# Four blocks of a depthwise convolution on 128x32 stationary tiles with time-shifted copies

## The reference, cut to what matters

```python
def causal_dwconv(x, w, b):
    width, ch = w.shape
    y = lax.conv_general_dilated(
        x, w[:, None, :].astype(x.dtype), window_strides=(1,),
        padding=((width - 1, 0),), dimension_numbers=("NWC", "WIO", "NWC"),
        feature_group_count=ch)
    return y + b

def conformer_conv(u, b_glu, w_dw, b_dw, ln_g, ln_b):
    u = u + b_glu
    a, gate = jnp.split(u, 2, axis=-1)
    v = a * jax.nn.sigmoid(gate)
    v = causal_dwconv(v, w_dw, b_dw)
    v = layernorm(v, ln_g, ln_b)
    return jax.nn.silu(v)
```

## Time and profile before

| | before |
|---|---|
| time, median of 3 runs | 1257.6 us (1256.13 to 1257.68) |
| span of the profiled execution | 1251.5 us, 19242 instructions |
| PE busy | 1209.8 us, 97% |
| DVE busy | 894.0 us, 71% |
| ACT busy | 639.7 us, 51% |
| POOL busy | 14.0 us, 1% |
| granted TensorE clock, mean | 0.995 |

### The profile page before, as it was taken

One profiled execution on the slowest core, in us unless ns is written; L12 is line 12 of the kernel. 1 busy time (PEld: TensorE's weight loads), 2 busy tenths in 40 slices (PEclk: granted clock), 3 DMA queues, 4 the chain that ended last, 5 costly groups with the idle time before them and its releaser, 6 DMA issues.

```text
span 1251.5 us, 19242 instructions
## 1 busy us (share of the span) xinstructions
PE 1209.8 (97%) x7928; PEld 1092.5 (87%) x7928; DVE 894.0 (71%) x1369; ACT 639.7 (51%) x1017; POOL 14.0 (1%) x32
## 2 busy tenths in 40 slices
PE   6999899999999999999999999999999999999997
PEld 6988798999989869899998978878798989999885
DVE  5996678877776666788778856665576647677664
ACT  6564555555464435555555334435444555555553
POOL 0000000000000000000000000000000000000000
PEclk9999999999999999999999999999999999999999
DMA  9520435555443323465454544544454732223341
GB/s 387 220 101 1 168 135 174 213 186 187 183 169 123 105 86 126 157 214 198 174 201 137 205 164 157 205 168 146 173 186 174 259 147 102 102 102 102 135 178 58
DMA packets 28710, 200.52 MB, mean 160 GB/s; under 512 B 3408, under 2 KB 3536, under 8 KB 5072
## 3 DMA queue, kind: packets, MB, share of 16 engines
q1 hardware_dynamic: 28624, 199.30, 43.8%
HBM read 198.24 MB, written 1.05 MB: 159 GB/s over the span
## 4 chain that ended last, share of the span: by engine, by line
PE 80%; DVE 11%; ACT 5%; issue 3%; DMA 1%; DVEq 0%; POOLq 0%; ACTq 0%; POOL 0%; SPq 0%
PE bank L726 22%; PE bank L727 22%; PE bank L728 22%; DVE WL L1616 4%; ACT WH L1236 3%; PE bank L874 2%; DVE work L1808 2%; PE bank L1210 1%; PE bank L1193 1%; PE bank L1107 1%; PE bank L860 1%; DVE work L1761 1%; DVE work L1757 1%; PE bank L937 1%; PE bank L1184 1%
## 5 line engine op out<-in xcount | busy, mean ns | idle before, releaser
L1616 DVE TENSOR_TENSOR WL<-RAW,WH 128x2048 fp32r<-128x2048 f32 x180 | 411.5, 2289 | 151.2 <-ACT WH L1236 150.1
L1236 ACT ACTIVATE WH<-RAW 128x2048 fp32r<-128x2048 f32 x180 | 343.2, 1910 | 208.5 <-PE bank L728 202.8
L726 PE MATMUL bank<-XH,WH 128*128 128x256 f32 x1264 | 361.9, 286 | 18.1 <-DVE WL L1828 12.0
L727 PE MATMUL bank<-XL,WH 128*128 128x256 f32 x1264 | 358.6, 284 | 0.0
L728 PE MATMUL bank<-XH,WL 128*128 128x256 f32 x1264 | 358.5, 284 | 0.0
L726 PEld LDWEIGHTS bank<-XH,WH 128*128 128x128 f32 x1264 | 243.4, 193 | 22.5 <-DVE XL L1821 11.9
L727 PEld LDWEIGHTS bank<-XL,WH 128*128 128x128 f32 x1264 | 243.4, 193 | 0.5
L728 PEld LDWEIGHTS bank<-XH,WL 128*128 128x128 f32 x1264 | 243.4, 193 | 0.0
L726 PE MATMUL bank<-WH,MH 128*128 128x512 f32 (+1 forms) x544 | 199.7, 367 | 5.7 <-DVE WL L1616 3.8
L727 PE MATMUL bank<-WL,MH 128*128 128x512 f32 (+1 forms) x544 | 196.7, 362 | 0.0
L728 PE MATMUL bank<-WH,ML 128*128 128x512 f32 (+1 forms) x544 | 196.6, 361 | 0.0
(11 more groups left out here) (275 smaller groups left out, 1507.0 us busy)
## 6 DMA issues: line engine op xcount, KB each, us to landing
RAW<-wstream SPq DMA_DIRECT2D x181, 1024.0 KB, 4.8
con<-consts SPq DMA_DIRECT2D x1, 1681.0 KB, 13.2
work<-xT_in SPq DMA_DIRECT2D x1, 1024.0 KB, 4.9
x<-x_in SPq DMA_DIRECT2D x1, 1024.0 KB, 11.0
work<-mem_in SPq DMA_DIRECT2D x1, 1024.0 KB, 16.3
xn<-memT_in SPq DMA_DIRECT2D x1, 1024.0 KB, 11.9
par<-params SPq DMA_DIRECT2D x1, 858.0 KB, 14.2
gfree<-g_final SPq DMA_DIRECT2D x1, 512.0 KB, 17.0
```

Source lines behind the costliest of these rows:

```text
L726: mm(o, ah, bh, start=start, stop=False)
L727: mm(o, ah, bl, start=False, stop=False)
L1236: act_fn(WH[:, t % RING, :], RAW[:, t % RING, :], ACT.Copy).then_inc(w_rounded, 1)
L1616: tt(WL[:, t % RING, :], RAW[:, t % RING, :], WH[:, t % RING, :].bitcast(F32), ALU.subtract).then_inc(w_split, 1)
```

## The change

Blocks 2 to 5 now go to TensorE in full, blocks 0 and 1 stay on VectorE (62 taps). The stationary tile is 128x32: for a group of 32 channels its 128 rows are four copies of these channels, the copy n shifted by n tokens, and it holds the four taps 4m to 4m+3 as four stacked 32x32 diagonals. A block takes eight such steps (m = 0 to 7; the 32nd tap is zero) for each of its four groups, so 32 matmuls, and 128 in all. The four groups of a block write the four quarters of the partitions of one bank. Within a step the groups follow each other, then comes the next step. Slot 0 does the whole of block 2, the other six slots half a block each.

The shifted copies are made by DMA from `vpad` (`shift`), 16 DMAs of 32 partitions x 572 columns for each pair of blocks, one pair into MH, ML, the other into XH, XL. The SP queue issues them between the loads of weight tiles, behind waits on a new semaphore `glu_done`, the second pair also behind TensorE's use of XH in `qm`. The stationary tiles are made by GpSimd: four small additions form `pick`, and one `tensor_tensor` of 128x1024 for each block (`conv_weights`) multiplies it by the taps from the parameter array, whose part `w_rep` replaces four blocks of `w_dw_a`. They lie in the place of the diagonals, in `gfree` and in `xn`. The two `rms` of GpSimd now stand between them. ScalarE builds no diagonals, and takes the four convolution results out of PSUM with the bias (`conv_outs`). The mean takes the blocks in the order 2, 3, 4, 0, 1, 5. The load of `gfree` moves to the first tile of the second block.

```diff
-PE_CONV = {3: CONV // 2, 4: CONV, 5: CONV}
-PE_TAPS = [(b, k) for b, n in PE_CONV.items() for k in range(n)]
-TAPS_PER_SLOT = 11
+PE_BLOCKS = (2, 3, 4, 5)
+SHIFTS = 4
+GROUPS = 4
+STEPS = 8
+DIAG = P // SHIFTS
+VREP = 2 * (CONV - 1 + T)
+CONV_SLOTS = {0: [(2, 0), (2, 1)], 1: [(3, 0)], 2: [(3, 1)], 3: [(4, 0)], 4: [(4, 1)], 5: [(5, 0)], 6: [(5, 1)]}
...
+            def shift(j):
+
+                sp.wait_ge(glu_done, j)
+                for n in range(SHIFTS):
+                    for g in range(GROUPS):
+                        at = 2 * j * (CONV - 1 + T) + n
+                        sp.dma_start(shifted(j, g)[DIAG * n:DIAG * (n + 1), :], vflat[DIAG * g:DIAG * (g + 1), at:at + VREP])\
+                            .then_inc(shifts_loaded[j - 1], 16)
...
+                if TILES[t] == ("mk", 1):
+                    shift(1)
+                if TILES[t] == ("o0", O0_ORDER[0]):
+                    sp.wait_ge(w_used, TILE[("qm", 0)] + 1)
+                    shift(2)
+                if TILES[t] == FOX_FIRST[0]:
+
+                    sp.wait_ge(w_used, TILE[("o0", O0_ORDER[-1])] + 1)
                     sp.dma_start(gfree[:, :], g_final.partition_broadcast(P)).then_inc(gf_loaded, 16)
...
-            for n in (1, 0):
-                rms(n)
+            pool.wait_ge(ident_loaded, 16)
+            link(nc.gpsimd.tensor_tensor(pick[:, :], ident[:, 0:DIAG], ident[:, DIAG:2 * DIAG], ALU.add))
...
+            def conv_weights(b):
+
+                n = GROUPS * STEPS
+                taps = col("w_rep", PE_BLOCKS.index(b) * n, n)
+                nc.gpsimd.tensor_tensor(conv_w[b], pick[:, :].unsqueeze(1).to_broadcast([P, n, DIAG]),
+                                        taps.unsqueeze(2).to_broadcast([P, n, DIAG]), ALU.mult).then_inc(conv_w_built, 1)
+
+            rms(1)
+            pool.wait_ge(par_loaded, 16)
+            pool.wait_ge(front_lo, KD)
+            conv_weights(2)
+            rms(0)
+            conv_weights(3)
+            pool.wait_ge(front_lo, 2 * KD)
+            conv_weights(4)
+            conv_weights(5)
...
-                for n in range(slot * TAPS_PER_SLOT, (slot + 1) * TAPS_PER_SLOT):
-                    b, k = PE_TAPS[n]
-                    if k == 0:
+                for b, part in CONV_SLOTS[slot]:
+                    j = b // 2
+                    if part == 0:
                         conv_out[b] = take(("cv", b))
-                    last = k == PE_CONV[b] - 1
-                    pe.wait_ge(diag_built, n + 1)
-                    mm(conv_out[b][:, 0:T], diag[:, n % DIAGS, :], vpad[:, b, k:k + T], start=(k == 0), stop=last)\
-                        .then_inc(aux_done if last else diag_used, 1)
+                        pe.wait_ge(conv_w_built, PE_BLOCKS.index(b) + 1)
+                        if b % 2 == 0:
+                            pe.wait_ge(shifts_loaded[j - 1], 16 * SHIFTS * GROUPS)
+                    for m in range(STEPS // 2 * part, STEPS // 2 * (part + 1)):
+                        for g in range(GROUPS):
+                            at = (b % 2) * (CONV - 1 + T) + SHIFTS * m
+                            last = mm(conv_out[b][DIAG * g:DIAG * (g + 1), 0:T], conv_w[b][:, g * STEPS + m, :],
+                                      shifted(j, g)[:, at:at + T], start=(m == 0), stop=(m == STEPS - 1))
+                    if part == 1:
+                        last.then_inc(aux_done, 1)
...
-            for at, b in enumerate((0, 1, 4, 2, 3, 5)):
-                pe.wait_ge(*dve_a.next())
+            for at, b in enumerate((2, 3, 4, 0, 1, 5)):
+                if b in PE_BLOCKS:
+                    is_free(pe, ("cv", b))
+                else:
+                    pe.wait_ge(*dve_a.next())
...
+            def conv_outs(slot):
+
+                for b, part in CONV_SLOTS.get(slot, []):
+                    if part == 1:
+                        ready(act, ("cv", b))
+                        free(act_fn(conv[:, b, :], B(("cv", b))[:, 0:T], ACT.Identity, bias=col("b_dw_a", b)), ("cv", b), "act")
...
-            TAPS_IN_SLOT = 10
+            TAPS_IN_SLOT = 4
             dve_taps = [(b, i) for i in range(CONV) for b in (0, 1)]
-            dve_taps += [(b, i) for i in range(CONV) for b in (2, 3) if not 0 < i <= PE_CONV.get(b, 0)]
```

More of the change, by code:

```diff
@@ L384, in program @@
         hmask = sb("hmask", [P, 2])
+        pick = sb("pick", [P, DIAG])
         WORK = 10464
@@ L432, in program, with shifted @@
         z = wk(8448, NMB, T)
-        DIAGS = TAPS_PER_SLOT
-        diag = wk(8448, DIAGS, P)
+        xn_flat = xn[:, :, :].rearrange("p i d -> p (i d)")
+        conv_w = {b: v.rearrange("p (n c) -> p n c", c=DIAG)
+                  for b, v in zip(PE_BLOCKS, (wk(8448, 1024), gfree[:, :], xn_flat[:, 0:1024], xn_flat[:, 1024:2048]))}
+        def shifted(j, g):
+            part = (MH, ML)[g // 2][:, 0:6, :] if j == 1 else (XH, XL)[g // 2][:, :, :]
+            at = (g % 2) * VREP
+            return part.rearrange("p a t -> p (a t)").bitcast(F32)[:, at:at + VREP]
         fy = wk(0, 2, 4 * T)
@@ L508, in program @@
         ms_done = sem("ms_done")
-        diag_built = sem("diag_built")
-        diag_used = sem("diag_used")
+        glu_done = sem("glu_done")
+        shifts_loaded = [sem("shifts_loaded1"), sem("shifts_loaded2")]
+        conv_w_built = sem("conv_w_built")
         rstd_done = sem("rstd_done")
@@ L665, in halved @@
                 nc.gpsimd.tensor_tensor(rhalf[:, n, :], rstd[:, n, :], half[:, :], ALU.mult).then_inc(half_done, 1)
-            for n in (1, 0):
-                rms(n)
+            pool.wait_ge(ident_loaded, 16)
+            link(nc.gpsimd.tensor_tensor(pick[:, :], ident[:, 0:DIAG], ident[:, DIAG:2 * DIAG], ALU.add))
+            for n in (2, 3):
+                sync()
+                link(nc.gpsimd.tensor_tensor(pick[:, :], pick[:, :], ident[:, n * DIAG:(n + 1) * DIAG], ALU.add))
+            sync()
+            def conv_weights(b):
[12 more added lines that the diff above has]
+            conv_weights(5)
             pool.wait_ge(ln_var_done, 1)
@@ L1317, in attention @@
                             values(j)
-                    if base == 0 and s + 1 < n + 3:
-                        diags(s + 1)
+                    if base == 0:
+                        conv_outs(s - 1)
                     if s < n:
@@ L1848, in _ @@
                 else:
-                    ins.then_inc(dve_for_pe, 1)
+                    ins.then_inc(glu_done, 1)
+                    dve.wait_ge(glu_done, j)
                 if j == 0:
@@ L1874, in _ @@
                 dve.drain().then_inc(dve_for_pe, 1)
-            ready(dve, ("cv", 3))
-            dve.wait_ge(dve_chain, last_of[3])
-            free(tt(conv[:, 3, :], B(("cv", 3))[:, 0:T], conv[:, 3, :], ALU.add), ("cv", 3), "dve")
-            ready(dve, ("cv", 4))
-            free(ts(conv[:, 4, :], B(("cv", 4))[:, 0:T], col("b_dw_a", 4), None, ALU.add), ("cv", 4), "dve")
-            for n in range(3):
-                dve.drain().then_inc(dve_for_pe, 1)
-            ready(dve, ("cv", 5))
-            free(ts(conv[:, 5, :], B(("cv", 5))[:, 0:T], col("b_dw_a", 5), None, ALU.add), ("cv", 5), "dve")
-            dve.drain().then_inc(dve_for_pe, 1)
             pairs = [slice(2 * p, 2 * p + 2) for p in range(NMB // 2)]
@@ L2333, in param_array, with conv_taps_by_shift @@
     return np.ascontiguousarray(np.concatenate([v[n] for n, _ in PARAM_PARTS], axis=1))
+def conv_taps_by_shift(w):
+    out = np.zeros((SHIFTS * STEPS, 4 * P), np.float32)
+    out[0:CONV] = w[:, 2 * P:]
+    return out.reshape(STEPS, SHIFTS, 4, GROUPS, DIAG).transpose(1, 4, 2, 3, 0).reshape(P, 4 * GROUPS * STEPS)
 def channels(v):
```

28 lines of the change are left out of this document (10 added, 18 removed).

## The result

The changed kernel takes 1240.8 us (median of 4, 1239.57 to 1242.42) against 1257.6 us, a ratio of 0.9876 with a 95% interval of 0.9861 to 0.9891. So it is faster by 1.2%, 16.9 us; forecast were 5.7 us. The time is that of rival (A), 1240.5 us, though not all of (A)'s steps came out.

The account below looks back on a forecast made before the run. TensorE and VectorE were both taken to fill the slots. TensorE's 38.9 us against 45.3 saves 6.4, less 0.7 for VectorE's delay, 5.7: 1251.9 us against the median of 1257.6; 8-in-10 range 1238 to 1258.

Parts of the forecast that it names:

- rival (A): All four groups' tap matmuls run at once on TensorE: taps 13.8 us, VectorE's chain then binds, 1240.5 us; chance 0.27.
- the price of a tap instruction on TensorE: Convolution slots: 256 instructions, from 55.0 us without overlap of groups to 13.8 us with all four at once; 27.5 taken.
- the middle: TensorE's taps: each group costs one step, not two, 27.5 us in all; forecast 1251.9 us, chance 0.44.
- pairs side by side in the queue: Evidence from TensorE's rows that both instructions of one fp32 matmul are adjacent, held against all four groups overlapping.
- all of (A), the middle case but 0.04: How the chance of a result faster by more than 2.5 us was made up, given as 0.71.
- (C): GpSimd holds VectorE up between 18 and 55 us: 4 to 7 us of delay, 1256 to 1259 us; chance 0.12.
- GpSimd's delay of VectorE: GpSimd's tile building slows VectorE ahead of the slots: 0.7 us taken, bounds 0 and about 5 us.
- Tile-width changes: TensorE in the slots changes between 32 and 128 or 64 columns about eleven times more: 1.0 us, bounds 0 and 1.7.
- The SP queue: Thirty-two more DMA issues for shifted copies at 0.43 us each, 7 us for each pair, costed at nothing.
- `pick`: GpSimd's four small additions at 0.7 us each, through at 16.6 us, ahead of `rms(1)` at 17.24.
- A tile: One GpSimd stationary tile for a block: low end 1.2 us, in time even at 8 us; 2.2 us by the skill.
- "Either alone" against "both": In the slots before the change TensorE and VectorE are both full, so both have to be relieved.

Follow-up runs that it names:

- g_outer: Changed kernel with the tap matmuls reordered: within each half block one group goes through all its steps, then the next; 1258.1 us.
- no_slot_taps: Changed kernel without VectorE's last 16 taps, those in slots 0 to 3; 1239.5 us, ratio 0.9863.
- pool_early: Changed kernel with all four of GpSimd's stationary tiles made ahead of 35 us; 1239.0 us, ratio 0.9858.
- pool_late: Changed kernel with GpSimd's tiles for blocks 4 and 5 made later, behind a wait on a weight split; 1241.0 us, ratio 0.9878.
- no_pool_late: Changed kernel with GpSimd's tiles for blocks 4 and 5 left out; median 1238.1 us, ratio 0.9858.

## Why the prediction was wrong, and where it was right

**The failed step is the price of a tap instruction on TensorE.** The prediction took "the middle": the second instruction of a group "has the same quarter as the first and must follow it, but the first of the next group has another quarter and can start with it", so each group one step, 0.107 us an instruction, 27.5 us in all. The first half holds (the second instructions start 0.22 us after the first). What is wrong is what it was taken to mean: the next group doesn't have to stand behind the waiting second instruction. The price is 0.054 us, the lower bound, 13.8 us in all; the 13.7 us between are more than the whole error of 11.1 (1251.9 against 1240.8). On the other side stand 2.7 us more of delay in front of the slots, 1.7 of waiting and 0.5 for tile widths in them, and 2.5 lost behind the mean; the 4.5 us that only the medians show came on top, and 0.4 are left over. The evidence that I set against (A), pairs side by side in the queue, was true and beside the point, since position in the queue alone doesn't set the order of starts between quarters; g_outer's rows show it. The bounds were right, and the point between them was chosen by a story and not by a row. The range of 1238 to 1258 us holds the result only because (A) had been let into it. In the chances, "all of (A), the middle case but 0.04" is 0.67 and not 0.71; the 0.04 between are the rest of (C), which that sentence leaves unsaid.

The two statements of the Trainium skill come out accordingly (TensorE: Matmul & The Clock Gate, Part 3). Three column tiles 2.38 times as fast: four are here 0.215 / 0.054 = 4.0 times as fast. That matmuls start in program order the rows of g_outer contradict: an ML instruction at 73.91 us is ahead of an MH one at 74.12 that precedes it.

**(A)'s own steps.** It put TensorE's need at 25 us: measured 25.3. It put the mean near 96 us from VectorE's chain: it was 98.97, held by the late start and TensorE's own work, with VectorE's part 1.9 us (no_slot_taps). It took 17.1 us off the profiled span's end; 14.9 came at the mean and 12.4 at the end. That its 1240.5 us was met by the median is partly an accident of the base: the prediction added 6.1 us around the span for both kernels, while the difference of span and time is about 2 us and the rest was the short profiled execution of before.

**GpSimd's delay of VectorE was mis-sized**, 0.7 us taken of bounds 0 to 5: measured 3.4 us at the first slot, and about 4.3 if the weight tile had been split no earlier than before, so rival (C)'s 4 us. The prediction named the place, the split in front of the wait at 50.8 us, and its test ("no later than now by more than 1 us, else (C)") fired: 1.83 us. What it lacked is that the tile at 31 us is in the way as well, and that a longer wait of TensorE brings 3.4 us at half clock, 1.6 us more. (C) alone would have eaten the gain only beside the middle case; beside (A) it takes a fifth.

The rows fit an exclusive turn, not a shared pace. The Trainium skill (SBUF — State Buffer, "Who interferes with whom") says that a VectorE operation with two SBUF inputs and a GpSimd one that reads SBUF block each other fully, and whoever starts first goes on. The six taps at 52.40 us and the six at 46.10 one by one (shortest, median and longest in ns):

```profile
L1862 DVE SCALAR_TENSOR_TENSOR work<-work,par x6: 475/476/2125, 52.4 to 56.0; 128x256 f32<-128x256 f32 x6
```

```profile
L1862 DVE SCALAR_TENSOR_TENSOR work<-work,par x6: 477/478/480, 46.1 to 48.1; 128x256 f32<-128x256 f32 x6
```

A shared pace would stretch several taps a little; here one tap takes 2.13 us and the others their usual 0.48. Worked through: GpSimd's third tile, begun at 46.26 us, seems to get nothing done beside the six taps; it then runs, and ends near 50.3. The split at 49.08 is blocked until then, 50.3 + 2.3 = 52.6, where it ended at 52.5. The fourth tile goes from there to 54.24, and the tap at 52.40 waits for it, 1.65 us. The trace agrees to 0.2 us, and each tile costs VectorE at most its own 1.9 us. What stays open is who gets the turn between two taps: the tile at 31.29 us got in, the one at 46.26 did not.

**The smaller steps.** Tile-width changes: 0.14 us against 0.09, 1.5 us in all and inside the bounds. The SP queue, first pair and second:

```profile
42.92 1.84 SPq L625 DMA_DIRECT2D MH<-work  x2
44.81 1.22 SPq L625 DMA_DIRECT2D ML<-work  x2
...
60.13 2.47 SPq L625 DMA_DIRECT2D XH<-work  x2
```

An issue costs 0.61 us, not 0.43, and the first of a pair more, so 10.7 and 11.3 us for the two pairs and not 7; TensorE waits for no shift and no tile behind them, so the cost of nothing was right. `pick` was through at 14.5 us, ahead of the forecast 16.6, and `rms(1)` came at 17.1 us as forecast. A tile takes 1.92 us, within 1.2 to 8; the Trainium skill's 2.2 us (GPSIMD Engine Reference, section 3.1), an estimate from its figure for 2048 columns, was near. "Either alone" against "both": right, shown by the three kernels without taps. ScalarE: right; the 1.7 us that TensorE waits for its exponentials come from VectorE's taps in front of the maximum, so VectorE stayed on the path, as (A) had it, at a cost of 1.9 us.

## What to carry to other kernels

Where a price lies between two bounds a factor of four apart, let no story pick the middle: a row of the same pattern or a range that gives both ends their weight. Small matmuls on different column quarters should alternate, with at most four instructions of one quarter in a row (two fp32 matmuls). Work put on GpSimd isn't free even when it is early and small: look for what VectorE does with two inputs beside it, and for whether TensorE waits for that; a longer wait of TensorE can cost again in clock what it cost in time. And compare the profiled execution with the median before using its span as the base.

## What the runs showed of the hardware that I had not expected

Four column quarters run fp32 matmuls fully beside each other, 0.054 us for each instruction of 256 columns against 0.215, and instructions of different quarters start out of program order; with eight of one quarter in a row 0.127 us. GpSimd and VectorE's two-input work took turns: one tap of six took 2.13 us and the others 0.48. Relieving TensorE of 49 taps without relieving VectorE made the time no better, as the granted clock fell to 0.50 for up to 6.8 us at a time behind idle stretches (mean 0.984). Ahead of the slots a wait of TensorE of 3.61 to 3.63 us was followed by a stretch at half clock in all seven traces that have it; of the waits of 2.49 to 2.51 us two came with one (pool_early, pool_late) and one did not (no_pool_late), and behind the 1.29 us of before there was none.
